# A scan's decay-weighted values: eight scaled copies by ACT, one a head, where DVE had one product (first pass)

## The reference

```python
kv_chunk = jnp.einsum('bhnjd,bhnj,bhnjv->bhndv', kc, to_end, vc)
total = jnp.exp(cum[..., -1])
def step(s, inp):
    kv_n, tot_n = inp
    return tot_n[..., None, None] * s + kv_n, s
y_inter = jnp.einsum('bhnid,bhni,bhndv->bhniv', qc, jnp.exp(cum), s_before)
return (y_intra + y_inter)
```

## Time and profile before

| | |
|---|---|
| median of 3 runs | 2524.29 us (2523.5 to 2526.97) |
| profiled execution | 2524.43 us |
| its span, first to last instruction | 2522.6 us |
| busy over the span | PE 94%, DVE 47%, ACT 30%, POOL 9% |
| granted PE clock, mean | 0.982 |
| first pass of this scan | about 977 to 1036 us |

### The profile page before, as it was taken

The page is one execution under the profiler, slowest core; times in us unless marked ns, Lnnn a source line. Parts: engine busy times, 40 slices in busy tenths (PEclk is TensorE's granted clock), DMA queues, the critical chain, the costliest instruction groups (busy, mean ns, idle before and its releaser), DMA issues.

```text
span 2522.6 us, 30573 instructions
## 1 busy us (share of the span) xinstructions
PE 2378.9 (94%) x12716; PEld 1741.5 (69%) x12716; DVE 1181.0 (47%) x1953; ACT 744.3 (30%) x1287; POOL 224.8 (9%) x207
## 2 busy tenths in 40 slices
PE   7998999999998998899999999999998888999998
PEld 6783463333344988647888888877777767788886
DVE  3247332111364677835443433444566573544444
ACT  2235111111132434314112111123555563322222
POOL 0000011111103106200000000000202031000000
PEclk9999999999999999899999999999999999999999
DMA  9947749898511211222112212212001011233221
GB/s 342 360 144 255 257 169 380 321 367 332 190 26 35 68 51 43 92 83 67 51 51 84 67 51 67 67 51 61 30 1 55 17 68 53 91 99 100 91 88 72
DMA packets 177961, 308.86 MB, mean 122 GB/s; under 512 B 18459, under 2 KB 85395, under 8 KB 177696
## 3 DMA queue, kind: packets, MB, share of 16 engines
q1 hardware_dynamic: 164720, 278.40, 31.8%
q0 software_dynamic: 12368, 26.35, 3.0%
q10 hardware_dynamic: 736, 2.15, 0.2%
HBM read 355.05 MB, written 18.93 MB: 148 GB/s over the span
## 4 chain that ended last, share of the span: by engine, by line
PE 59%; DVE 9%; ACT 4%; issue 1%; DMA 0%; POOL 0%; DVEq 0%; ACTq 0%
PE PS L140 37%; PE PS L2544 11%; PE PS L2482 2%; PE PS L152 2%; PE PS L3131 2%; DVE X L110 2%; DVE Rr L110 1%; PE PS L3052 1%; PE PS L2488 1%; DVE H L110 1%; ACT X L130 1%; PE PS L2420 1%; DVE MIX L110 1%; DVE gate L110 1%; DVE H L118 1%
## 5 line engine op out<-in xcount | busy, mean ns | idle before, releaser
L140 PE MATMUL PS<-at,wH 128*128 128x512 f32 (+1 forms) x2144 | 563.8, 352 | 2.1 <-DVE at L110 2.1
L140 PEld LDWEIGHTS PS<-at,wH 128*128 128x128 f32 x2144 | 378.8, 190 | 57.0 <-issue 1.6
L140 PE MATMUL PS<-at,rest 128*128 128x512 f32 (+1 forms) x1072 | 376.6, 351 | 0.0
L2544 PE MATMUL PS<-wH,ac 128*128 128x512 f32 x880 | 277.9, 393 | 3.3 <-DVE hn L110 3.3
L110 DVE TENSOR_TENSOR rest<-ring,wH 128x2048 fp32r<-128x2048 f32 x66 | 150.4, 2291 | 211.2 <-ACT wH L133 210.6
L140 PEld LDWEIGHTS PS<-at,rest 128*128 128x128 f32 x1072 | 202.9, 189 | 27.2
L133 ACT CAST wH<-ring 128x2048 fp32r<-128x2048 f32 x66 | 124.6, 1906 | 264.5 <-PE PS L2544 199.8
L2544 PEld LDWEIGHTS PS<-wH,ac 128*128 128x128 f32 x880 | 165.2, 188 | 43.0 <-DVE hn L110 8.5
L2544 PE MATMUL PS<-rest,ac 128*128 128x512 f32 x440 | 171.4, 389 | 0.0
L140 PE MATMUL PS<-HI,ATr 128*128 128x256 f32 x512 | 148.6, 290 | 5.2 <-DVE MIXr L110 4.7
L140 PE MATMUL PS<-ring,AT 128*128 128x512 f32 x320 | 141.7, 599 | 0.8 <-ACT AT L133 0.8
(11 more groups left out here) (386 smaller groups left out, 4162.7 us busy)
## 6 DMA issues: line engine op xcount, KB each, us to landing
R<-in_w_gate_up_dram SPq DMA_DIRECT2D x32, 1024.0 KB, 11.2
ring<-in_w_down_dram SPq DMA_DIRECT2D x32, 1024.0 KB, 12.9
ring<-in_w_gate_up_dram SPq DMA_DIRECT2D x32, 1024.0 KB
ring<-in_w_ffn_gate_dram SPq DMA_DIRECT2D x22, 1024.0 KB, 5.4
ring<-in_w_ffn_up_dram SPq DMA_DIRECT2D x22, 1024.0 KB, 5.4
ring<-in_w_ffn_down_dram SPq DMA_DIRECT2D x22, 1024.0 KB, 5.0
ring<-in_w_ada_dram SPq DMA_DIRECT2D x16, 1024.0 KB, 7.4
HIw<-in_w_gate_up_dram SPq DMA_DIRECT2D x16, 1024.0 KB, 8.5
```

The costliest lines, as they stand in the source:

```text
L140: ins = self.e.matmul(out, l, r, start=k == 0, stop=k == len(pairs) - 1)
L2544: ins = p.e.matmul(bk(4 + n_dn % 3), a_, b_, start=start and i == 0, stop=stop and i == len(terms) - 1)
```

## The change

In the first pass the weighted product of chunks 0 to 4 goes from DVE to ACT: for each chunk eight instructions of 128x64, one a head, each a plain function (Identity) with a column of `ws` as its scale. ACT does chunk 0's before the first shift, and chunk i + 1's at the head of its iteration i, before that chunk's decay. They have a counter of their own, `weighted_a`, and PE's `update` waits for that in the first pass; DVE's counter `weighted_s` now counts only the second pass. The buffers, the values and everything of the second pass stay.

```diff
+     pe_high=("mixed_T_copy", 16), weighted_a=("expanded", 10), wq_high=("sq_z", 6), ...
@@ ssd_pe, update
-            p.wait_ge(S("weighted_s"), q + 1)
+            p.wait_ge(*((S("weighted_a"), q + 1) if i < 6 else (S("weighted_s"), q - 4)))
@@ ssd_act
+        def weighted(i):
+            t = ORDER[i]
+            a.wait_ge(S("kv_s"), i - 1)
+            for h in range(8):
+                a.fn(vws[(i + 1) % 2][:, 64 * h:64 * h + 64], xval(t)[:, 64 * h:64 * h + 64], ACT.Identity,
+                     inc=S("weighted_a") if h == 7 else None, scale=ws[:, t, 8 + h:9 + h])
+
+        weighted(0)
         shift(0)
         decays(0)
@@ 
         for i in range(12):
+            if i < 4:
+                weighted(i + 1)
             if i < 5:
                 decays(i + 1)
@@ ssd_dve
-            if n == 0:
+            if i == 6:
                 weighted(i)
@@
-            if n < 4:
+            if i > 5 and n < 4:
                 weighted(i + 1)
```

More of the change, by code:

```diff
@@ L70 @@
     q_pe_high=("cqb_copy", 4), k_pe_high=("ck_copy", 6), v_take=("kp_raw", 2), cq_high=("xb_copy", 12), ck_high=("z_silu", 6),
-    pe_high=("mixed_T_copy", 16), wq_high=("sq_z", 6), kv_high=("decay_exp", 6), mixed_T_copy=("mix_T_copy", 4),
+    pe_high=("mixed_T_copy", 16), weighted_a=("expanded", 10), wq_high=("sq_z", 6), kv_high=("decay_exp", 6), mixed_T_copy=("mix_T_copy", 4),
     xb_copy=("h1_T_copy", 8), cq_copy=("z_copy", 12), cqb_copy=("cq_copy", 4), ck_copy=("g_silu", 12), kp_copy=("conv_silu", 8),
```

## The result

| | before | the change |
|---|---|---|
| median, first comparison (13 runs each) | 2524.49 us | 2516.82 us |
| ratio | | 0.9977, 95% interval 0.9969 to 0.9984 |
| lowest and highest | 2520.41 to 2526.97 | 2514.54 to 2521.73 |
| profiled execution's span | 2522.6 | 2519.4 |
| DVE, ACT busy (whole span) | 1181.0, 744.3 | 1171.6, 753.2 |

What follows compares the result with a forecast made beforehand. DVE was taken to bound the first pass, PE next. Chunk 2's mixed product at 1000.5 plus periods 9.86, 9.51 and 8.73 gave 1028.6 against 1033.34, -4.75 us: 2519.5 us, range 2517.2 to 2522.8.

Steps and rivals of the forecast that it cites:

- DVE's beat: First pass, periods between mixed products: 12.16 to 9.86, 11.81 to 9.51, 8.73 unchanged; one of two POOL waits goes.
- ACT's price: Eight 128x64 copies a chunk on ACT take 2.0 us, bounds 1.2 and 2.7, far bound 5.8.
- The head: Chunk 0's copies stand ahead of the first shift, so the pass starts 2.0 us later.
- Chunk 2 over ACT: Copies between PE's z block and the decay put chunk 2's mixed product at 1000.5, against 1000.64 before.
- DVE's own time: Chunk 2's mixed product without ACT's chain: 1000.0, through PE's late scores for chunk 1 and POOL's product.
- The end of the pass: Chunk 5's mixed product at 1028.6 against 1033.34, -4.75 us; its own product on PE and the end move the same.
- rival 1: Copies don't overlap or PE stays at half clock longer: gain only 3.35 us, 2520.9; chance 0.20.
- the sum: Chunk 2's 1000.5 plus periods 9.86, 9.51 and 8.73 gives 1028.6, -4.75 us; forecast 2519.5 us.
- faster by over 0.2%: Outcome class for the whole kernel, made of rival 3 and the lower part of the forecast's range; chance 0.35.
- 2: POOL's wait comes back at the sum into y or the mixed product: gain only 1.6 us, 2522.7; chance 0.13.
- 3: PE becomes the bound, DVE waits for nothing: -6.5 us, 2517.8; chance 0.12.
- 4: ACT becomes the bound in every chunk, from 4.5 us of copies; at 5.8, +5.3 us, 2529.6; chance 0.05.

Runs made afterwards that it cites:

- pool_half: The kernel before, with POOL's masks made for four of the eight heads only; 2514.27 us, ratio 0.9953.
- one_copy: The changed kernel with one of the eight copies a chunk, the weighting of the other seven heads left out; 2519.4 us, ratio 0.9976.
- twice: The changed kernel with the eight copies of each chunk made twice, nothing left out; 2522.86 us, ratio 0.9995.
- early: The changed kernel with chunk 0's product back on DVE and ACT's copies of chunks 1 to 4 made a step earlier; 2516.65 us, ratio 0.9966.
- keep: The changed kernel with 23 useless matmuls in PE's idle time ahead of chunk 0's own product; 2515.23 us, ratio 0.9963.
- again: The changed kernel once more, unchanged, for a second trace; 2515.69 us.
- again2: The changed kernel once more, unchanged, for a third trace; 2515.87 us.
- before_again: The kernel before once more, unchanged, for a second trace; 2522.64 us, ratio 0.9992.
- before_3: The kernel before once more, unchanged, for a third trace; 2523.45 us, ratio 0.9997.
- head_dve: The changed kernel with only chunk 0's product back on DVE, chunks 1 to 4 staying on ACT; 2517.14 us, ratio 0.9970.
- early_keep: The version early with 23 useless matmuls in PE's idle time ahead of chunk 0's own product; 2515.22 us, ratio 0.9969.
- best: The version early with PE's z block 5 ahead of chunk 0's own product and the last block ahead of the product with the state; 2516.50 us, ratio 0.9963.

## Why the prediction was right, and where it was off

- *DVE's beat.* 12.16 was to become 9.86, 11.81 to become 9.51, 8.73 to stay: measured 9.87, 9.50, 8.73 in the first trace, within 0.02 of that in the other two. The reason, that one of two waits for POOL goes with the product, is shown by the decay's 1.47 and by pool_half.
- *ACT's price.* Eight copies were to take 2.0: 2.00 to 2.02. The head was to come 2.0 later: 1.91.
- *Chunk 2 over ACT.* Forecast 1000.5, that is 32.4 from the mark: 32.80, 32.07, 32.34. DVE waits for ACT there in the change, and one_copy and twice move it. What I gave as DVE's own time, 1000.0 or 31.9, holds too: early, without ACT in the way and with the head 1.9 earlier, comes to 29.90, so the change would have been at 31.8 by DVE alone; keep has 31.77. ACT decides there, but by no more than 0.3 to 1.0.
- *The end of the pass.* Forecast for the mixed product of chunk 5 -4.75: from the mark -4.33, -5.05 and -4.79. Its own product was to follow 3.49 behind, and did in two traces of three; in the first 5.79, by the half-clock stretch of rival 1, which I had placed at the head and not at chunk 4. There I had only looked at whether PE would be late, not at what its wait of 2 us does to the clock.
- *The time.* Forecast -4.75; the traces from the mark to the end give -4.9 on average, the ratio of the first comparison -5.8 (-7.8 to -4.0), the others more. So the size was at the low side, if the time is asked and not the traces. The step that I would name is the sum: it has no term for how PE's half-clock stretches are spread over an execution, and the 0.35 for "faster by over 0.2%" looks too low, since all three ratios lie beyond it (of their intervals only the third's does so whole). Three traces of each kernel show no place outside the pass that gains in each of them. The granted clock goes some way to the rest: in again and again2 it is 0.9846 on average, in the executions of before next to them 0.983, and at the 2.4 us for 0.001 above these 0.0015 would be 3 to 4 us, an estimate, which leaves some 5 of the 8.4 us between their means. Further executions of before, in before_again and before_3, had 0.9841, so the difference in clock isn't the change's doing as far as these runs tell; what brings it stays open.
- *Rivals.* 1: the copies do overlap (one alone takes 0.33, eight 2.00), so that half was wrong; a further stretch at half clock did come, in one trace of three, and cost 2.3 where I had 1.8. 2: not in the change, where the sum into y takes 0.69; but in keep POOL's wait did come back, at the mixed product. 3: no; chunk 4's own product came near where I had put it, 54.9 to 55.7 from the mark (in the first trace 1024.12 - 968.47; forecast 1024.0 - 968.11 = 55.9), but it followed DVE's mixed product by 3.5 each time, and the last one stood at 63.7 at best and not at 62.2: DVE kept the beat. 4: no; twice shows ACT with 4.1 a chunk, just below the 4.5 that I had worked out as the point, still hidden, and its trace and ratio still not slower than before.

## What to carry to other kernels

An instruction that takes longer in one place than its like elsewhere may be waiting for something inside itself: find what ends when it ends, and price its removal by that, not by its own length. When DVE and POOL both read two on-chip tensors in the same stretch, look at POOL's program before moving DVE's, since much of the time may be there (here 2.35 of the 3.73 us of two instructions). Don't put copies made by another engine at the head of a chain: it cost 1.9 us here. Making them ahead of that engine's next wait rather than behind it (early) took ACT's wait away and gained nothing more, since the next to decide stood at the same place.

## What the runs showed of the hardware that I had not expected

- PE stood idle 2.07 us ahead of the same product in nine traces (the three of the change, one_copy, twice, head_dve, early, keep and early_keep). In three of them it fell to half clock behind it: the change's first (1027.8 to 1034.6, clock 0.50), keep (the product itself takes 2.04) and head_dve (the product still takes 1.10, then 0.50 from 1024 to 1026); in six it didn't. The idle time alone doesn't tell whether it falls: it fell after 2.83 us in best and after 3.00 in twice (0.50 granted from 990 to 992); and not after 0.44 in keep and 0.53 in early_keep. It costs 2.3 us here, and makes a single execution of no use for a change of this size.
- DVE's mixed product, let go while POOL starts an instruction of 1.90, took 2.97 (1.23 alone): 1.74 of POOL's 1.90 is paid by DVE.
- The idle 0.48 on DVE that no releaser explains sits at one place of DVE's program for each kernel: at t1 in before (and before_again, before_3 and pool_half), two instructions later in the change. In these and in again, one_copy and twice the DMA queue of kind "instruction" (q14) moves one packet in the 4 us around it. In head_dve, early and best I don't find the idle time, though head_dve has such a packet between 1004 and 1006 and early between 1006 and 1008, at the same point of the pass. So a packet alone doesn't bring it, and that it is DVE's own instructions arriving is not shown.
